# TensorE's layer loop written out, the first two chunks of the first up stage one behind the other, and the third chunk rounded ahead of the first silu

## The reference

```python
def swiglu_half(x, w1, w3, w2):
    return 0.5 * ((jax.nn.silu(x @ w1) * (x @ w3)) @ w2)

for l in range(DEPTH_2):                     # 2 layers
    x = layer_norm(ALPHA * x + swiglu_half(x, ffn1_w1[l], ffn1_w3[l], ffn1_w2[l]), ln1_g[l], ln1_b[l])
    h = x @ w_in[l]
    ...                                      # spatial gating, gated delta rule, gated linear attention
    x = layer_norm(ALPHA * x + mix, ln2_g[l], ln2_b[l])
    x = layer_norm(ALPHA * x + swiglu_half(x, ffn2_w1[l], ffn2_w3[l], ffn2_w2[l]), ln3_g[l], ln3_b[l])
```

## Time and profile before

| | |
|---|---|
| median of 3 runs | 2934.55 us (2932.45 to 2935.44) |
| profiled execution, its own time | 2935.26 us |
| its span | 2933.5 us |
| TensorE busy | 2866.6 us, 98% of the span |
| VectorE, ScalarE, GpSimd busy | 40%, 38%, 29% |
| mean granted TensorE clock | 0.990 |

### The profile page before, as it was taken

How to read it: one execution, slowest core, us unless ns; L and a number is a source line. 1 busy time by engine, 2 the same in 40 slices (tenths; PEclk the granted TensorE clock), 3 DMA queues, 4 the chain that set the end, 5 groups by cost and what they waited for, 6 DMA issues and landing times.

```text
span 2933.5 us, 48552 instructions
## 1 busy us (share of the span) xinstructions
PE 2866.6 (98%) x20016; PEld 2369.0 (81%) x20016; DVE 1177.2 (40%) x1478; ACT 1124.4 (38%) x1312; POOL 836.7 (29%) x314
## 2 busy tenths in 40 slices
PE   8999999999999999999999999999999999999997
PEld 6787887787888888788888887888888788888886
DVE  3655643632322152543622324332152543632315
ACT  3557554422233245532333324333245531433224
POOL 4122213412101535362000163110544362110053
PEclk9999999999999999999999999999999999999999
DMA  5111112222222432100222232222332200122233
GB/s 182 44 67 71 56 46 73 73 100 87 100 89 98 143 110 101 73 2 31 74 99 100 95 136 102 100 100 95 134 115 96 86 3 31 58 100 100 100 129 115
DMA packets 36533, 257.63 MB, mean 88 GB/s; under 512 B 4080, under 2 KB 4128, under 8 KB 6432
## 3 DMA queue, kind: packets, MB, share of 16 engines
q1 hardware_dynamic: 34848, 249.66, 23.8%
q0 software_dynamic: 1536, 5.83, 0.6%
HBM read 253.31 MB, written 2.16 MB: 87 GB/s over the span
## 4 chain that ended last, share of the span: by engine, by line
PE 91%; DVE 3%; POOL 2%; ACT 2%; issue 2%; DMA 0%; ACTq 0%; DVEq 0%; POOLq 0%
PE ps L2279 50%; PE ps L1780 6%; PE ps L1735 5%; PE ps L1772 4%; PE ps L2429 3%; PE ps L2481 3%; PE ps L1079 2%; PE ps L2324 2%; PE ps L1065 1%; PE ps L1866 1%; POOL wl L1385 1%; PE ps L1851 1%; PE ps L1837 1%; PE ps L1790 1%; ACT wh L1993 1%
## 5 line engine op out<-in xcount | busy, mean ns | idle before, releaser
L1385 POOL TENSOR_TENSOR wl<-raw,wh 128x2048 fp32r<-128x2048 f32 x116 | 533.1, 4595 | 740.5 <-ACT wh L1993 740.2
L2279 PE MATMUL ps<-xh,wh 128*128 128x512 f32 x1584 | 621.2, 392 | 7.7 <-DVE wl L2102 4.8
L2279 PE MATMUL ps<-xl,wh 128*128 128x512 f32 x1584 | 616.8, 389 | 0.0
L2279 PE MATMUL ps<-xh,wl 128*128 128x512 f32 x1584 | 616.4, 389 | 0.0
L1993 ACT ACTIVATE wh<-raw 128x2048 fp32r<-128x2048 f32 x224 | 427.6, 1909 | 397.8 <-PE ps L2279 309.6
L2102 DVE TENSOR_TENSOR wl<-raw,wh 128x2048 fp32r<-128x2048 f32 x110 | 281.3, 2558 | 553.9 <-ACT wh L1993 551.2
L1956 POOL TENSOR_TENSOR hl<-hf,hh 128x1024 f32 x44 | 105.8, 2405 | 906.0 <-ACT hh L2003 906.0
L2279 PEld LDWEIGHTS ps<-xh,wh 128*128 128x128 f32 x1584 | 297.3, 188 | 80.2 <-issue 8.6
L2279 PEld LDWEIGHTS ps<-xh,wl 128*128 128x128 f32 x1584 | 297.4, 188 | 62.6
L2279 PEld LDWEIGHTS ps<-xl,wh 128*128 128x128 f32 x1584 | 297.4, 188 | 60.5
L2279 PE MATMUL ps<-hh,wh 128*128 128x512 f32 x704 | 276.9, 393 | 1.6 <-POOL wl L1385 1.2
(11 more groups left out here) (375 smaller groups left out, 4592.2 us busy)
## 6 DMA issues: line engine op xcount, KB each, us to landing
raw<-stream SPq DMA_DIRECT2D x232, 1024.0 KB, 4.8
btw<-bias_rows POOLq DMA_DIRECT2D x2, 1536.0 KB, 8.2
x<-x_in SPq DMA_DIRECT2D x4, 512.0 KB, 5.6
out<-x SPq DMA_DIRECT2D x4, 512.0 KB, 2.6
sgp<-sg POOLq DMA_DIRECT2D x2, 640.0 KB, 4.1
cst<-consts SPq DMA_DIRECT2D x1, 1108.0 KB, 9.3
c<-bias_consts SPq DMA_DIRECT2D x1, 1024.0 KB, 14.7
bt<-bias_rows POOLq DMA_DIRECT2D x2, 512.0 KB, 9.2
```

The lines of the kernel that those rows point to most:

```text
L1385: nc.gpsimd.tensor_tensor(wl[:, p, :], raw[:, p, :], wh[:, p, :].bitcast(F32), ALU.subtract).then_inc(s["chunk_lo"], 1)
L2279: mm = te.matmul(dst, wslice(w, k), r(k), start=(start and m == 0), stop=(stop and m == len(steps) - 1))
```

## The change

Three edits. (1) TensorE's loop over the layers is a loop of Python, so that its program holds both layers one behind the other, with constants in all waits; the inner loops over chunks stay. (2) In layer 0 alone, chunks 0 and 1 of the first up stage are made one behind the other by `first_apart`; chunk 0 waits for `evac[0]` and its own rest, chunk 1 for `evac[1]` and its own. (3) ScalarE's first step of each up stage is taken out of its loop, and in it chunk 2 is rounded ahead of the silu of chunk 0.

```diff
-            def up(l, w, i, off):
+            def up(l, w, i, off, first=False):
                 n = c_no(l, off) + i * 2
                 act.wait_ge(s["chunk_used"], n + 1)
 
+                if first:
+                    round_chunk(n + 2, 0)
                 act.wait_ge(evac[1], n_evac(l, 1, off) + i)
                 ac.activation(silu_t[:, :, :], ps[:, 0:2, :], ACT.Silu).then_inc(evac[0], 1)
-                round_chunk(n + 2, 0)
+                if not first:
+                    round_chunk(n + 2, 0)
...
-                with act.Fori(0, UP // 2) as i:
+                up(l, 0, 0, OFF_UP1, True)
+                with act.Fori(1, UP // 2) as i:
                     up(l, 0, i, OFF_UP1)
...
-                with act.Fori(0, UP // 2) as i:
+                up(l, 1, 0, OFF_UP2, True)
+                with act.Fori(1, UP // 2) as i:
                     up(l, 1, i, OFF_UP2)
...
+            def first_apart(off):
+
+                n = c_no(0, off)
+                ready = normed(0, 0)
+                for p in range(2):
+                    pe.wait_ge(evac[p], n_evac(0, p, off))
+                    pe.wait_ge(s["chunk_lo"], n + p + 1)
+                    for k in range(KT):
+                        if p == 0:
+                            ready(k)
+                        for j in range(2):
+                            c = 256 * k + P * j
+                            for a, (w, r) in enumerate(((wh, xh), (wh, xl), (wl, xh))):
+                                mm = te.matmul(ps[:, 2 * p + j, :], w[:, p, c:c + P], r[:, k, :], start=(k == 0 and a == 0), stop=(k == KT - 1 and a == 2))
+                    mm.then_inc(s["chunk_used"], 1)
...
-            with pe.Fori(0, LAYERS) as l:
-                first_two(l, OFF_UP1, normed(l, 0))
+            for l in range(LAYERS):
+                if l == 0:
+                    first_apart(OFF_UP1)
+                else:
+                    first_two(l, OFF_UP1, normed(l, 0))
```

## The result

| | before | changed |
|---|---|---|
| median | 2934.55 us (2932.45 to 2935.44) | 2917.69 us (2914.65 to 2919.42) |
| profiled execution, its own time | 2935.26 us | 2918.20 us |
| its span | 2933.5 us | 2916.2 us |

The ratio is 0.9942, 95% interval 0.9930 to 0.9953: faster by 0.58%, and the interval excludes a ratio of 1. The forecast was 2917.8 us.

The account below looks back on a forecast made before the run. TensorE, busy 98% of the span, bounds the kernel, so gains come from its waits and lower clock. 8.5 + 5.2 + 2.6 + 0.5 = 16.8 us off 2935.26, less 0.7 for the median, gives 2917.8 us; range 2913.5 to 2922.5.

Parts of the forecast that it names:

- Layer 0's first two chunks, 8.5 us: Layer 0's first up stage: both waits and the low clock go, chunk 2 starts at 721.0, not 729.53: 8.5 us.
- Start of layer 1, 5.2 us: Layer 1's first up stage: branch's 3.75 us goes, late parameters leave about 1.6 us of wait at chunk 2: 5.2 us gained.
- my last sign of being wrong: Forecast is wrong if the lower clock shows in stretches where the norm's small matmuls stand; no size given.
- hardly matters: Layer 1's start: whether the clock stays low counts little, since the wait of about 1.6 us at chunk 2 absorbs it.
- One reading: Layer 1's norm with no branch at its end: behind its 0.82 us wait the clock didn't fall in the stretch read.
- Second up stages, 2.6 us: Third chunk of both layers' second up stages: rounding first makes rest and silu 0.9 us early, winning 1.3 us each.
- The third edit in the first up stages: First up stages: a table load ahead of the rounding makes the edit worth less than 1.3 us there.
- Table loads in the inner loops, nothing: Inner loops: 40 silus lose their table load, but TensorE isn't waiting for them, so no gain.
- The rest, 0.5 us: Register instructions ahead of TensorE's waits go: between nothing and 1.2 us at some four places, taken as 0.5 us.
- No drain behind a rounding ahead of a table load: ScalarE: load starts 0.01 us behind rounding, costs 1.28 us. Drain rival: 1.3 us more per non-first load, 2921.2 us, chance 0.05.
- A rival's price: Layer 0's entry: the next wait takes the old one's place, at worst all 8.5 us lost, 2926.3 us, chance 0.04.
- The branch: Branch back over the layer costs 3.75 us. Slower rival: each inner loop entry costs as much plus clock, 2961 us, chance 0.02.

Follow-up runs that it names:

- c1: The changed kernel measured once more, unaltered, on one chip with another variant: 2917.31 us, ratio 0.9940 to the kernel before.
- e1: The changed kernel with layer 0's first two chunks interleaved again, the other two edits kept: 2927.85 us, ratio 0.9970.
- e8: The changed kernel with other bodies of TensorE's up-stage inner loops (192 or 480 matmuls, or no loop in layer 1's first): 2918.37 us, ratio 0.9943.
- e2: The changed kernel with the silu ahead of the rounding again in every step: 2922.06 us, ratio 0.9956.
- e3: The kernel before with the third edit alone (rounding ahead of the silu in ScalarE's first step): 2931.24 us, ratio 0.9985.
- e6: The changed kernel with the parameter wait behind ScalarE's first up step and ScalarE's layer loop written out: 2914.87 us, ratio 0.9933.
- e4: The kernel before with only TensorE's layer loop written out: 2931.22 us, ratio 0.9987.
- e5: The changed kernel with ScalarE's wait for the layer's parameters moved behind its first up step: 2915.67 us, ratio 0.9935.
- c2: The changed kernel with the later parameter wait and ScalarE's layer loop written out, measured once more: 2916.51 us, ratio 0.9938.
- e7: The changed kernel with the later parameter wait and the first two chunks one behind the other in both layers: 2919.41 us, ratio 0.9946.

## Why the prediction was right

The time came out as forecast, 2917.7 for 2917.8 us, and most of it by the steps named. That it fits to 0.1 us is luck: executions of the same program go from 2914.65 to 2919.42 us. In the profiled one the stages named gave 8.6 + 4.5 + 2.7 = 15.8 us, 0.5 less than forecast, and the stretches between them 1.71 - 0.55 = 1.2 us (705.21 to 703.50 and 707.26 to 707.81 in the table). In c1, the same program, those stretches took 2.0 us more than before.

- *Layer 0's first two chunks, 8.5 us*: 30.56 to 21.99 us, 8.6. Both waits and the low clock are gone, and e1 brings them back (0.66 from 706 to 711 us). The margins held: chunk 1's rest and the parameters weren't waited for.
- *Start of layer 1, 5.2 us*: 34.21 to 29.72 us, 4.5; in c1 4.1. The mechanism was right: the branch gone, the parameters' landing late next. The size was off in two ways. The lower clock that came behind the old wait now lies over the norm's broadcasts and filling matmuls (0.76 over 7 us), so the first matmul came 6.40 us behind `lncol` instead of 5.81 (my last sign of being wrong, which came true and cost little); and from the landing to chunk 2 it took 5.92 us (1814.17 to 1820.09), not 5.6, because 0.24 us lie between the landing and ScalarE's first load (1814.41), where I had 0.1, and 0.14 us between the silu's end and the matmul, where I had 0.05. That the low clock "hardly matters" there was half right: it delays the norm itself, and with it the load of the parameters. e8 has the same program in this place, but for the entry to the inner loop that no wait of either shows, and full clock over the norm (1.00 from 1790 to 1797 us): the first matmul comes 5.90 us behind `lncol`, the parameters are asked for 0.5 us sooner and land in 2.8 us, and the stage takes 29.00 us, which is the 5.2 us. One reading was empty: the stretch of the earlier trace rows that ends at 2186.00 lies ahead of the 0.82 us of wait behind which I said the clock didn't fall. The trace bears it out (1.00 from 2186.4 to 2196.4 us).
- *Second up stages, 2.6 us*: 1.32 + 1.37 = 2.7 us; e2 and e3 each show the same by themselves.
- *The third edit in the first up stages*: it was to be worth 0.9 us where a load stands ahead of the rounding. It is 0.6 to 0.7 us in e3, 1.0 us at layer 1 in the changed kernel (counted from the parameters' landing, against e2), and nothing in layer 0, as predicted.
- *Table loads in the inner loops, nothing*: e2 bears it out.
- *The rest, 0.5 us*: can't be told. The waits at L1092 for VectorE fell from 2.3 to 1.7 us, and those in the mixers without a releaser were 0.5 + 0.4 us and are 0.8. The stretches between the stages differ by more than this.
- *No drain behind a rounding ahead of a table load*: e6's rows have the load 0.01 us behind the rounding's end, and in the changed kernel it is 0.02. What the Trainium skill says of a drain (ScalarE: Activation LUTs, section "What ACT_TABLE_LOAD costs") isn't seen here. By its figure of 1.38 us, an estimate, layer 1's chunk 2 would have come up to 2.8 us later than it did.
- *A rival's price*: without layer 0's gain I had 2926.3 us as "just within or beyond 0.2%". It is 0.28% below the kernel before, so beyond.
- *The branch*: e8 and e1 show that neither an entry to a loop (0.1 us) nor a branch back over 480 matmuls costs what the one over the layer did. That fits what the Trainium skill states (Runtime: NRT & Kernel Launch, section on instruction fetch mechanics): only a target that is no longer held has to be fetched. The packets on q8 in e8 agree.

The forecasts for the parts were less good than the sum. The medians of e1 and e4 came out 2.4 and 1.7 us above, their profiled executions 3.1 and 5.4 us. Both traces put most of this outside of what was changed. The column "then to L0 second up" is the same program on TensorE in the changed kernel, e1, e2, e5 to e8, c1 and c2 (except for the inner loop's form in e8), and goes from 703.33 to 706.52 us. It follows the clock. By the traces' clock records the lower level was granted for 13.7 us of this stretch in the changed kernel, e2, e5, e6 and e8, and for 20.5 us in e1, e7, c1 and c2. The former took 703.3 to 703.6 us, but e8 705.4, and the latter 706.1 to 706.5 us. Of e8's excess 1.0 us is a wait without a releaser at L1079, which the others don't have there. The changed kernel and c1, the same program, show where, first the former, then the latter:

```profile
1266.00:1290.00 24.00, 20.50 (x653) 20.33 (x649) 7.58 (x13) 9.56 (x17) 23.84 (x21) 0.93 0.01 3
...
1363.00:1400.00 37.00, 37.00 (x214) 29.63 (x213) 17.43 (x20) 7.34 (x8) 5.14 (x4) 0.95 0.16 58
```

```profile
1266.00:1290.00 24.00, 20.42 (x606) 20.24 (x602) 7.09 (x13) 8.50 (x15) 23.13 (x20) 0.86 0.01 2
...
1363.00:1400.00 37.00, 37.00 (x209) 30.03 (x208) 16.31 (x18) 8.20 (x9) 5.14 (x4) 0.91 0.16 55
```

Over the mixer's small matmuls (1266 to 1290 us) the clock was at 0.93 once and 0.86 the other time. Where small matmuls with 2 and 128 columns stand between those of the output stage (1363 to 1400 us) it was at 0.95 and 0.91. The mean clock times the length gives 24 x 0.07 + 37 x 0.04 = 3.2 us at full clock that were missing; the column differs by 2.9 us. So 3 us come and go with no change in the program, and that is the size of the terms of a part like e4. Why one execution has more of the lower clock than another isn't settled: no run here controls it.

## What to carry to other kernels

Price a wait together with what is late next: the branch back over the layer was 3.75 us and 1.65 us of clock, and 4.5 us remained, since the next load hung on the norm and not on TensorE. An order of two streams is good or bad by which one arrives late: one chunk behind the other wins where the second weight chunk is late (layer 0, 7.9 us) and loses where the input tiles are (layer 1, 3.3 us). Where a gain is small against the spread, cut the trace at the same instructions in both kernels: here the stages repeat within 0.1 us, but for layer 1's first one, which hangs on a DMA (29.72 and 30.15 us), while the whole differs by 3 us.

## What the runs showed that I had not expected

- A first step taken out of a loop changed where table loads are put: one came ahead of a plain copy at the head of ScalarE's loop (1.28 us on the path), 40 went from the inner loops; with ScalarE's layer loop written out as well, the one at the head went too.
- TensorE waited 2.1 us and not 4.7 in e7, although six matmuls of 1.36 us stand against a tile every 2.04 us. A row's idle time leaves out 0.16 us each time, and the second matmul behind each wait starts another 0.1 us late. The stage's 3.9 us above its work (25.75 against 21.86 us from the first matmul to chunk 2) is the true count, still less than 4.7.
- The load of the parameters took 2.8 to 3.6 us from issue to landing in layer 1, 2.2 to 2.3 us in layer 0. As layer 1's chunk 2 hangs on it, this spread goes straight into the stage.
